# The last layer's modulation of the second block: dot products on VectorE behind the feed-forward part, in place of products on TensorE

## The reference, cut to what matters

```python
mod   = jax.nn.silu(c)     @ w_mod[l] + b_mod[l]      # 1024 -> 6144, for the 256 tokens
mod_c = jax.nn.silu(c_ctx) @ w_mod[l] + b_mod[l]      # the same weights, for the 256 context tokens
sh1, sc1, g1, sh2, sc2, g2 = jnp.split(mod[:, None, :], 6, axis=-1)
sh1c, sc1c, g1c, sh2c, sc2c, g2c = jnp.split(mod_c, 6, axis=-1)
h  = x * (1 + sc1) + sh1
hc = xc * (1 + sc1c) + sh1c
y, yc = _token_mixers(h, hc, ...)
x = _layer_norm(DEEPNORM_ALPHA * x + g1 * y, ...)
h = x * (1 + sc2) + sh2
x = _layer_norm(DEEPNORM_ALPHA * x + g2 * _sq_relu_mlp(h, w_fc1[l], w_fc2[l]), ...)
```

## Time and profile before

| | us |
|---|---|
| median of three runs | 2104.78 (2096.36 to 2105.37) |
| the profiled execution | 2100.62 |
| its span | 2098.8 |
| TensorE busy | 1906.4 (91%) |
| VectorE busy | 1019.7 (49%) |
| ScalarE busy | 756.9 (36%) |
| ring chunks moved | 403 of 1 MB |
| the 32 steps of `ffn0` in this execution | about 1260 to 1644 |

### The profile page before, as it was taken

The page is one execution under the profiler, slowest core; times in us unless marked ns, Lnnn a source line. Parts: engine busy times, 40 slices in busy tenths (PEclk is TensorE's granted clock), DMA queues, the critical chain, the costliest instruction groups (busy, mean ns, idle before and its releaser), DMA issues.

```text
span 2098.8 us, 24684 instructions
## 1 busy us (share of the span) xinstructions
PE 1906.4 (91%) x10104; PEld 1331.0 (63%) x10104; DVE 1019.7 (49%) x1676; ACT 756.9 (36%) x1200; POOL 112.6 (5%) x152
## 2 busy tenths in 40 slices
PE   6988799999898999999979879999999897988997
PEld 3654555555575555557535646777777573578997
DVE  1483532323445323256467554444444665655665
ACT  1154243423242434243256434222222323644433
POOL 0590000000000000000000011000000100010000
PEclk9999899999999999999979989999999897989999
DMA  9668499999556999992200112435344131024430
GB/s 393 249 253 323 158 403 400 409 407 365 221 210 250 371 416 421 421 374 80 81 21 1 40 41 94 187 123 191 148 158 183 40 121 40 1 81 159 180 144 21
DMA packets 61705, 429.14 MB, mean 204 GB/s; under 512 B 6544, under 2 KB 9744, under 8 KB 9872
## 3 DMA queue, kind: packets, MB, share of 16 engines
q1 hardware_dynamic: 61584, 427.46, 51.6%
HBM read 426.38 MB, written 1.05 MB: 204 GB/s over the span
## 4 chain that ended last, share of the span: by engine, by line
PE 76%; DVE 13%; ACT 8%; issue 1%; DMA 1%; SPq 0%; DVEq 0%; POOL 0%; ACTq 0%
PE bank L293 15%; PE bank L297 11%; PE bank L299 10%; PE bank L298 10%; PE bank L1008 10%; PE bank L996 7%; PE bank L332 3%; DVE ring_halves L2333 2%; ACT work_halves L2327 2%; PE bank L2006 2%; ACT work_halves L928 2%; PE bank L1983 2%; DVE ring_halves L935 2%; PE bank L2345 1%; DMA ring<-in_ws_dram 1%
## 5 line engine op out<-in xcount | busy, mean ns | idle before, releaser
L297 PE MATMUL bank<-work_halves 128*128 128x512 f32 (+1 forms) x1344 | 475.9, 354 | 35.8 <-DVE ring_halves L2333 10.0
L299 PE MATMUL bank<-work_halves,ring_halves 128*128 128x512 f32 (+1 forms) x1344 | 461.4, 343 | 0.0
L297 PEld LDWEIGHTS bank<-work_halves 128*128 128x128 f32 x1344 | 258.8, 193 | 92.1 <-issue 31.4
L298 PE MATMUL bank<-HH_halves,work_halves 128*128 128x512 f32 (+1 forms) x832 | 289.5, 348 | 0.0
L299 PEld LDWEIGHTS bank<-work_halves,ring_halves 128*128 128x128 f32 x1344 | 258.6, 192 | 29.1
L1008 PE MATMUL bank<-ring,work 128*64 128x512 f32 x1024 | 261.2, 598 | 0.4 <-ACT work_halves L1191 0.4
L2333 DVE TENSOR_TENSOR ring_halves<-ring,work_halves 128x2048 fp32r<-128x2048 f32 x72 | 164.5, 2287 | 54.2 <-ACT work_halves L2327 54.2
L293 PE MATMUL bank<-HH,ring 128*128 128x256 f32 x768 | 176.2, 389 | 16.0 <-DVE HH L473 6.6
L293 PEld LDWEIGHTS bank<-HH,ring 128*128 128x128 f32 x768 | 148.3, 195 | 49.3 <-issue 18.7
L298 PEld LDWEIGHTS bank<-HH_halves,work_halves 128*128 128x128 f32 x832 | 161.9, 195 | 20.0 <-issue 2.2
L298 PE MATMUL bank<-work_halves 128*128 128x512 f32 (+1 forms) x512 | 172.1, 336 | 0.0
(11 more groups left out here) (302 smaller groups left out, 2567.8 us busy)
## 6 DMA issues: line engine op xcount, KB each, us to landing
ring<-in_ws_dram SPq DMA_DIRECT2D x380, 1024.0 KB, 7.3
work<-in_ws_dram SPq DMA_DIRECT2D x23, 1024.0 KB, 9.3
con<-in_con_dram SPq DMA_DIRECT2D x1, 1204.0 KB, 15.7
XX<-in_xT_dram SPq DMA_DIRECT2D x1, 1024.0 KB, 11.9
XX<-in_cT_dram SPq DMA_DIRECT2D x1, 1024.0 KB, 15.3
out_dram<-XX SPq DMA_DIRECT2D x1, 1024.0 KB, 4.8
par<-in_par_dram SPq DMA_DIRECT2D x1, 338.0 KB, 3.0
con<-in_con_dram SPq DMA_DIRECT2D x1, 128.0 KB, 2.9
```

Source lines behind the costliest of these rows:

```text
L297: pe.matmul(out, l[0], r[0], start=start, stop=False)
L298: pe.matmul(out, l[0], r[1], start=False, stop=False)
L299: return pe.matmul(out, l[1], r[0], start=False, stop=stop)
```

## The change

`mods[3]` is no longer done by `Behind` but by a new class `Dotted`. Its chunks hold 256 whole columns of `w_mod[1]` laid in rows: partition `p` has columns `256 i + p` and `256 i + 128 + p`, 1024 floats each. One more chunk, `conds`, holds both conditions, the same on every partition. ScalarE takes their Silu into `work` (step 3). In steps 4 to 27 VectorE multiplies each column with a condition and sums along the free dimension, seeded with the bias, straight into `modt`: `tensor_tensor_reduce` at line 439, two columns a chunk, for both conditions in the first eight chunks and for one in the other sixteen, 32 + 32 = 64 in all. Each waits for the one before it. TensorE has no part in it.

```diff
-NCHUNK = 24 * 4 + 14 + 13 + 2 * 96 + 2 * 44
+NCHUNK = 24 * 4 + 1 + 14 + 13 + 2 * 96 + 2 * 44
...
+        class Dotted:
+            def __init__(self, M, which, l, at, first):
+                self.M, self.which, self.l, self.first = M, which, l, first
+                self.cond, self.prod = [work[:, at + 1024 * i:at + 1024 * i + 1024] for i in range(2)], work[:, at + 2048:at + 3072]
+            def begin(self, dve):
+                pass
+            def plan(self, i):
+                if i == self.first - 2:
+                    chunk(self.M.st, "conds")
+                if 0 <= i - self.first < 24:
+                    chunk(self.M.st, self.which, self.l, i - self.first)
+            def pe(self, pe, i):
+                pass
+            def act(self, act, i):
+                if i == self.first - 1:
+                    st = self.M.st
+                    loaded(act, ("conds",))
+                    for q in range(2):
+                        t = act.activation(self.cond[q], ring_of(("conds",))[:, 1024 * q:1024 * q + 1024], ACT.Silu)
+                    t.then_inc(st.act("used", ("conds",)), 1)
+            def dve(self, dve, i):
+                i -= self.first
+                if 0 <= i < 24:
+                    M, st, key = self.M, self.M.st, (self.which, self.l, i)
+                    loaded(dve, key)
+                    st.wait_ge(dve, "used", ("conds",))
+                    w = k8(ring_of(key), 1024)
+                    before = ("column", 2 * i - 1, M.n((i - 1) // 8) - 1) if i else None
+                    for a in range(2):
+                        for q in range(M.n(i // 8)):
+                            j = 2 * i + a
+                            if before:
+                                st.wait_ge(dve, *before)
+                            t = dve.tensor_tensor_reduce(self.prod, w[:, a, :], self.cond[q], 1.0, par_(M.bias, j), MUL, ADD, M.mod[:, j, q:q + 1])
+                            before = ("column", j, q)
+                            t.then_inc(st.dve(*before), 1)
+                    st.at["used", key] = st.at["mod", i // 8] = st.at[before]
...
-        mix0 = Mix(0, mods[2], Behind(k8(work[:, 13312:13824], 256), (mods[3], 0), (mods[3], 1), (mods[3], 2)))
+        mix0 = Mix(0, mods[2], Dotted(mods[3], "dot", 1, 13312, 4))
...
+        if n == "dot":
+            w = X["w_mod_2"][key[1]][:, 256 * key[2]:256 * key[2] + 256]
+            return w.T.reshape(2, P, 1024).transpose(1, 0, 2)
+        if n == "conds":
+            return np.broadcast_to(np.stack([X["c_2"].reshape(-1), X["c_ctx_2"].reshape(-1)]), (P, 2, 1024))
```

## The result

The changed kernel runs in 2071.15 us (median of 4, 2068.72 to 2073.96) beside 2103.95 us before: ratio 0.9859, 95% interval 0.9844 to 0.9874, so 26 to 33 us less. Its profiled execution took 2072.63 us with a span of 2070.8, against 2100.62 and 2098.8. 2077 had been predicted, in a range of 2069 to 2097.

The account below looks back on a forecast made before the run. TensorE was taken to bound the steps of ffn0; 27.0 us off it less 1.7 us of waits for VectorE gave 25.3 us, so 2075.3 from the profile or 2079.5 from the median; predicted 2077 us, range 2069 to 2097.

Parts of the forecast that it names:

- TensorE is the bound in the steps, and what it sheds comes off the time: Steps of ffn0: TensorE busy all 290 us from 1320 to 1610, so a microsecond less there is one less overall.
- 27.0 us off TensorE: Steps of ffn0: 22 background chunks of 1.18 us (26.0 us) and 3 turns of 0.35 (1.0 us) go.
- Two of the 24 chunks are worth nothing: Chunks of steps 0 and 1, before TensorE's 4.32 us gap: removing them only lengthens it, to 6.3 us.
- 1.35 us a dot product: VectorE, steps 4 to 27: each multiply-and-sum with its accumulator read takes 1.35 us; four take 5.4 us.
- 1.7 us of waits at steps 13 and 14: TensorE waiting for VectorE: 0.9 us for step 11's cut before step 13, 0.8 us for a tile's bank.
- the 7 us of cover: Kernel before, step 11: VectorE's cut ended at 1409.2 and was needed at 1416.2, 7 us that get spent.
- ScalarE's Silu and table loads, the queue, the extra MB are hidden: ScalarE: 3.4 us in step 3 and a table load before the final root; SyncE's queue: one more MB; all free.
- Sum 25.3: Whole kernel: 27.0 us off TensorE less 1.7 us of waits gives 25.3 us saved.
- A: VectorE in the dot-product steps: 1.6 us a dot product, 9 us of waiting, 2082.6 or 2087 us; chance 0.2.
- B: VectorE, mainly steps 4 to 11: two cycles an element, 2.45 us a dot product, 2116 us; chance 0.1.
- C: TensorE, steps 12 and 13 or more: short waits drop its clock, five cost 12 us, 2088 us; chance 0.08.

Follow-up runs that it names:

- experiment 1: Changed kernel with each dot product over 8 of its 1024 elements: step 2 to ffn0's closing squares 337.49 us against 338.22; median 2072.41 us.
- experiment 5: Kernel before with its background chunks two steps later (steps 2 to 31): step 2 to ffn0's closing squares 367.46 us against 365.15; median 2100.78 us, ratio 1.0000.
- Experiment 3: Changed kernel with eight dot products in place of four in each of the first eight chunks: 2115.37 us, ratio 1.0075 to the kernel before.
- experiment 2: Changed kernel with five dot products in place of four in each of the first eight chunks: 2083.28 us, ratio 0.9918 to the kernel before.
- experiment 9: Changed kernel, first eight chunks dealt to every third step, step 2's cut ahead of step 0's tiles in both feed-forward parts: 2060.83 us, ratio 0.9803 to before.

## Why the prediction was right

- *TensorE is the bound in the steps, and what it sheds comes off the time.* Right: TensorE lost 27.66 us of visible work (experiment 1) and the stretch 26.93.
- *27.0 us off TensorE: 22 chunks of 1.18, 3 turns of 0.35.* Right in kind, 0.7 too low: 1.20 and 0.42. Reading a pitch off three neighbouring starts gave 1.18; a difference over four whole steps is the better ruler.
- *Two of the 24 chunks are worth nothing.* Right: 2.3 us when they are moved to where they count (experiment 5), and the gap grew from 4.32 to 6.15.
- *1.35 us a dot product.* 1.33, and 1.21 for the last of a chunk, whose follower doesn't wait for it: 5.2 for four, where 5.4 stood. The sentence of the Trainium skill on halved throughput ("Vector Engine (DVE) Microarchitecture Reference", section 7, Points that are easy to get wrong), which is on the scalar-tensor-tensor form, does not carry over to this instruction: with both sources in SBUF and float32 it took 1284 ns for 1024 elements, beside 1224 for the plain two-input row. Experiment 3 shows what twice the time would have meant in steps 4 to 11 alone: 42 us more, and a kernel slower than before.
- *1.7 us of waits at steps 13 and 14.* The mis-sized term: 0.73 us. The places were right. The cut of step 11 ended at 1404.08 (1401.79 + 2.29), and the first weight load of step 13 waited 0.17 us for it; TensorE's passes lost less than 0.1 (predicted: 0.9). The third tile of step 13, the seventh counted from step 12, did wait for its bank, 0.21 us in the row and 0.16 more behind it (predicted 0.8). Counted again with 5.2 us for four dot products from step 6 on, the cut comes 0.1 us in time and the bank about 0.45 too late, so the 0.2 us counted too much make up most of the difference. That so little was waited is also luck: the 7 us of cover were spent to the last tenth, and experiment 2 shows that one more dot product a step brings 8.9 us.
- *ScalarE's Silu and table loads, the queue, the extra MB are hidden.* Right: the load at 1310.32 stands in ScalarE's idle time, the one at 1625.13 ends 3.4 us before TensorE's sum arrives.
- *Sum 25.3.* Measured 26.9 in the stretch: 0.7 from the prices, 1.0 from the waits. The median fell below the 2077 predicted by another 4 us that the stretch doesn't have. The repeat of the changed kernel gave 2074.57 beside 2101.15 for the kernel before, 26.6 us less, as in the stretch, and medians of the kernel before lie from 2100.15 to 2103.95. So this part looks like scatter.
- *Rivals.* A (1.6 us) and B (2.45 us) fall with the measured 1.33. C falls for these steps: the waits are 0.2 us, and in experiment 2 waits up to 2.7 us left the clock at 2.4 GHz. It isn't refuted in general: in the last layer the clock was at 1.2 GHz behind 2.4 us (experiment 9).

## What to carry to other kernels

Work that is moved from the bound engine to an idler one is paid for not by its mean load but by its longest crowded run: here a VectorE that was 78% busy had nothing left at one deadline, and one more operation a step cost 84% of itself, while the same work dealt out evenly was free. Count, step by step, when the operation behind the new work is due. And before pricing work that goes, look whether it stood in a gap: its place there was worth nothing, but the gap itself, with the slow clock behind it, was worth 8.7 us.

## What the runs showed of the hardware that was not expected

- The multiply-and-sum instruction takes 1284 ns for 1024 elements of two float32 sources in SBUF, 60 ns more than a plain two-input operation; its accumulator read takes 83 ns, about half of the 128x1 operation of the earlier trace rows (156 ns).
- TensorE's clock: in the steps of `ffn0` it stayed at 2.4 GHz behind waits of up to 2.7 us (experiment 2) and was at 1.2 GHz behind waits of 3.9 us and more (experiment 3). Behind the waits of 4.3 and 6.2 us in front of step 2, before and after, it was there for 4.7 us in both, so the longer gap cost nothing more at that place. But in the last layer it was at 1.2 GHz behind 2.4 us of waiting (experiment 9). So the length of the wait alone doesn't tell; what else decides stays open here.
- A wait of TensorE shows 0.16 us too short in the idle time, since the records of passes overlap by that much.
